# A hybrid decoder step on one core: projections summed over row quarters, h made by quarters, the last FFN round tile by tile

## The reference

```
mod = silu(c) @ w_ada + b_ada                      # c: 1 + 8 rows, w_ada 2048 x 12288
sh1, sc1, g1, sh2, sc2, g2 = split(mod, 6)
h = rmsnorm(x, g_pre_mix) * (1 + sc1) + sh1
z, xbc, dt, q, k, v = split(h @ w_in)              # 2048 x 5648
... conv and SSD mixer on z, xbc, dt; stick-breaking attention on q, k, v ...
m = concat(y, o) @ w_out                           # 2048 x 2048
x = x + g1 * rmsnorm(m, g_post_mix)
h = rmsnorm(x, g_pre_ffn) * (1 + sc2) + sh2
u = causal_conv(h @ w_ffn_in)                      # 2048 x 11264
f = (silu(gate(u)) * val(u)) @ w_ffn_out           # 5632 x 2048
x = x + g2 * rmsnorm(f, g_post_ffn)
```

## Time and profile before

| | us |
|---|---|
| median of three runs | 2014.4 (2013.41 to 2021.6) |
| profiled execution, time | 2012.36 |
| profiled execution, span from first to last instruction | 2010.4 |
| first projection product starts | 129.0 |
| output projection's last adaLN rows copied | 1077.4 |
| last product tile of the FFN added | 1975.0 |

### The profile page before, as it was taken

The page is one execution under the profiler, slowest core; times in us unless marked ns, Lnnn a source line. Parts: engine busy times, 40 slices in busy tenths (PEclk is TensorE's granted clock), DMA queues, the critical chain, the costliest instruction groups (busy, mean ns, idle before and its releaser), DMA issues.

```text
span 2010.4 us, 31591 instructions
## 1 busy us (share of the span) xinstructions
PE 1788.4 (89%) x13853; PEld 1584.5 (79%) x13853; DVE 942.2 (47%) x1212; ACT 653.1 (32%) x607; POOL 52.8 (3%) x146
## 2 busy tenths in 40 slices
PE   3869999997667887885997799999999999999986
PEld 2348998896545665453996799999999999999985
DVE  0052323323665332535234756566566566566554
ACT  1132222223633342113222543333333333333332
POOL 1000000000000000010000000000000000000001
PEclk9869999998678895587999899999999999999997
DMA  9966887884058993036674344444444454544431
GB/s 325 340 240 225 287 281 261 278 282 161 3 186 304 367 361 102 0 116 230 231 279 160 105 152 165 167 168 168 165 159 162 165 167 168 168 164 160 160 104 63
DMA packets 185180, 389.49 MB, mean 194 GB/s; under 512 B 9692, under 2 KB 18572, under 8 KB 184458
## 3 DMA queue, kind: packets, MB, share of 16 engines
q1 hardware_dynamic: 178816, 373.32, 53.8%
q0 software_dynamic: 2592, 10.42, 1.4%
q10 hardware_dynamic: 3634, 3.74, 0.6%
HBM read 377.03 MB, written 10.41 MB: 193 GB/s over the span
## 4 chain that ended last, share of the span: by engine, by line
PE 80%; DVE 9%; DMA 4%; ACT 4%; issue 2%; ACTq 1%; SPq 0%; POOL 0%; DVEq 0%; POOLq 0%
PE ps L667 20%; PE ps L668 20%; PE ps L669 20%; PE ps L623 4%; PE ps L642 4%; DMA araw<-in_w_ada_dram 2%; PE ps L864 2%; PE ps L735 1%; PE ps L1004 1%; ACTq L1163 1%; PE ps L897 1%; PE ps L631 1%; PE ps L995 1%; PE ps L1052 1%; DVE xraw L1676 1%
## 5 line engine op out<-in xcount | busy, mean ns | idle before, releaser
L1481 DVE TENSOR_TENSOR wlo<-raw,whi 128x2048 fp32r<-128x2048 f32 x192 | 438.2, 2289 | 441.3 <-ACT whi L1208 440.9
L1208 ACT ACTIVATE whi<-raw 128x2048 fp32r<-128x2048 f32 x192 | 367.0, 1915 | 665.1 <-PE ps L669 372.5
L667 PE MATMUL ps<-h2hi,whi 128*128 128x288 f32 x1408 | 416.7, 296 | 12.3 <-DVE wlo L1481 12.3
L668 PE MATMUL ps<-h2lo,whi 128*128 128x288 f32 x1408 | 417.4, 296 | 0.0
L669 PE MATMUL ps<-h2hi,wlo 128*128 128x288 f32 x1408 | 416.6, 296 | 0.0
L667 PEld LDWEIGHTS ps<-h2hi,whi 128*128 128x128 f32 x1408 | 268.2, 190 | 12.9 <-issue 11.9
L669 PEld LDWEIGHTS ps<-h2hi,wlo 128*128 128x128 f32 x1408 | 264.6, 188 | 0.0
L668 PEld LDWEIGHTS ps<-h2lo,whi 128*128 128x128 f32 x1408 | 264.5, 188 | 0.0
L667 PE MATMUL ps<-hhi,whi 128*128 128x288 f32 x704 | 211.5, 300 | 11.7 <-DVE wlo L1481 11.7
L667 PE MATMUL ps<-ghi,whi 128*128 128x288 f32 x704 | 209.0, 297 | 5.5 <-DVE wlo L1481 5.5
L668 PE MATMUL ps<-hlo,whi 128*128 128x288 f32 x704 | 210.5, 299 | 0.0
(11 more groups left out here) (373 smaller groups left out, 2122.1 us busy)
## 6 DMA issues: line engine op xcount, KB each, us to landing
raw<-in_w_ffn_in_dram SPq DMA_DIRECT2D x88, 1024.0 KB, 5.0
raw<-in_w_ada_dram SPq DMA_DIRECT2D x64, 1024.0 KB, 6.6
raw<-in_w_in_dram SPq DMA_DIRECT2D x44, 1024.0 KB, 8.5
raw<-in_w_ffn_out_dram SPq DMA_DIRECT2D x44, 1024.0 KB, 5.0
araw<-in_w_ada_dram SPq DMA_DIRECT2D x32, 1024.0 KB, 13.9
kring<-in_cache_k_dram SPq DMA_DIRECT2D x64, 512.0 KB, 5.8
vring<-in_cache_v_dram SPq DMA_DIRECT2D x64, 512.0 KB, 5.9
raw<-in_w_out_dram SPq DMA_DIRECT2D x16, 1024.0 KB, 5.8
```

What stands on the lines that cost most here:

```text
L667: mm(o, whi[:, high, q, cols], xh, start=(first and q == 0), stop=False)
L668: mm(o, whi[:, high, q, cols], xl, start=False, stop=False)
L1208: fn(whi[:, g % HIGH], raw[:, ring.slot[u]], ACT.Copy).then_inc(hi_ready, 1)
L1481: tt(wlo[:, slot], raw[:, slot], whi[:, g % HIGH].bitcast(F32), SUB).then_inc(lo_ready, 1)
```

## The change

- **Order of tiles.** 8 a, then four times (`ggaaa` five times and one g), 4 a, then `ggaaa` eight times, then g. The same 96 adaLN tiles and the same product tiles. `ADA_ORDER` sorts the first eight adaLN groups so that scale and shift of chunk quarter 0 come first, then those of quarter 1 and so on.
- **Products by row quarters.** The projection goes over all 11 groups with the rows of quarter 0, then of quarter 1, and so on (output projection: quarters 2, 3, 0, 1). Each product tile is complete in PSUM by itself. It uses two pairs of banks out of three (banks 0 to 5), p % 3; adaLN has bank 7 and the fold and the dt products bank 6. ACT copies the first quarter's pairs out, DVE adds the pairs of the three others into `proj` or `mT`.
- **h by quarters.** `hf` holds 4 chunks. Quarter 0 is made ahead of the first product, quarters 1 to 3 on DVE and ACT at adaLN tiles 16, 24 and 32; the dt products go along in four parts.
- **Start.** ACT issues c, x, then the vectors; POOL issues contexts, wdt and the rest. DVE's copies of the contexts come behind the norm.
- **Last round.** `ghi2`, `glo2` in buffers of their own; 16 tiles of one chunk each in banks 0 to 2; beside each the rows of x2 (x before the last sum, transposed), and gf = gain * f transposed; squares summed on DVE; then one multiply-add of rows with the norm's factor per token, and six stores on SP's queue.
- Some semaphores are merged; nothing else moves.

```diff
+    MIXER = ("ggaaa" * (PROJ_GROUPS // 2) + "g") * QUARTERS
+    OUTPUT = "ggaaa" * (QUARTERS * OUT_GROUPS // 2)
-    ring = Ring("a" * FIRST + "ggaa" * (PROJ // 4) + "a" * BETWEEN + "ggaa" * (RING * KC // MC // 2) + "g" * (3 * RING * FC // MC),
+    ring = Ring("a" * FIRST + MIXER + "a" * BETWEEN + OUTPUT + "g" * (3 * RING * FC // MC),
                 FIRST, WIDE, DEEP, (FIRST, BEFORE_OUT))
+    ADA_ORDER = [g for q in range(QUARTERS) for g in (QUARTERS + q, q)] + list(range(2 * QUARTERS, 6 * QUARTERS))
...
+            def product(x):
...
                 pe.wait_ge(lo_ready, g + 1)
                 for m in range(MC):
+                    p = 2 * g + m // 2
+                    if m % 2 == 0 and p >= 3:
+                        pe.wait_ge(*evacuated(p - 3))
+                    o = ps[:, 2 * (p % 3) + m % 2, 0:T]
+                    cols = slice(m * P, (m + 1) * P)
+                    for q in range(QC):
+                        xh, xl = x(product_of(g)[0] * QC + q)
+                        mm(o, whi[:, high, q, cols], xh, start=(q == 0), stop=False)
+                        mm(o, whi[:, high, q, cols], xl, start=False, stop=False)
+                        i = mm(o, wlo[:, slot, q, cols], xh, start=False, stop=(q == QC - 1))
...
+            def quarter(p):
+                dve.wait_ge(mod_ready, 2 * (p + 1))
+                c.link(stt(gainT[:, part], modT[:, SC1 + 4 * p:SC1 + 4 * p + 4, :], 1.0, vec, ADD, MUL))
+                if p:
+                    dve.wait_ge(dt_full, p)
+                    dve.wait_ge(h_hi, p)
+                    dve.wait_ge(h_lo, p)
+                tt(hf[:], xT[:, part], rT[:].unsqueeze(1).to_broadcast([P, QC, T]), MUL).then_inc(xr_ready, 1)
...
+                dve.wait_ge(h_hi, p + 1)
+                tt(hlo[:, part], hf[:], hhi[:, part].bitcast(F32), SUB).then_inc(h_lo, 1)
...
+            for kind in MIXER:
+                if kind == "a":
+                    ada(a)
+                    a += 1
+                else:
+                    q, g = product_of(n)
+                    if n + 1 < QUARTERS * PROJ_GROUPS:
+                        lo()
+                    if q:
+                        for i in range(2):
+                            from_psum(proj[:, MC * g + 2 * i:MC * g + 2 * i + 2, :], n, i)
+                    n += 1
...
+            for j in range(KC):
+                f_tile(j)
+                if j == 0:
+                    conv_rows()
+                if 1 <= j <= 12:
+                    if j == 1:
+                        pe.wait_ge(fc_o, 2)
+                    x2_rows(j - 1)
+                if j >= 3:
+                    gf_rows(j - 3)
+            for k in range(KC - 3, KC):
+                gf_rows(k)
...
+            for t in range(NT + 1):
+                w = P if t < NT else TS
+                r = rtok[0:w, t:t + 1]
+                early, late = x2tok[0:w, t, 0:DM - GC], x2tok[0:w, t, DM - GC:DM]
+                stt(early, gtok[0:w, t, :], r, early, MUL, ADD).then_inc(y_ready, 1)
+                stt(late, ps[0:w, 5 + t, :], r, late, MUL, ADD).then_inc(y_ready, 1)
```

More of the change, by code:

```diff
@@ L444, in _ @@
             sp.wait_ge(dtE_full, SC)
[L445 to L451, removed]
-            for i in range(KC // MC):
-                pair(w_out_v, i * GC, after_states if i == 0 else (lambda j: None))
+            for i in range(BETWEEN):
+                ada()
+            for half in range(2):
+                sp.wait_ge(hn_dma[half], 16 * (NB // 2))
+            for kind in OUTPUT:
+                if kind == "a":
+                    ada()
+                else:
+                    q, g = product_of(pos.g)
+                    load(rows(w_out_v, q, g * GC))
+                    pos.g += 1
             def fo(r):
@@ L645, in ada_unit @@
                 pos.u += 1
-            def adaq(bank, fold_last=True):
-                pe.wait_ge(group_free, pos.group + 1)
-                if fold_last:
-                    fold(bank)
-                for j in range(RING):
-                    ada_unit(bank, j)
                 pos.ada += 1
-            def unit3(bank0, xs, first, last, before=lambda m: None):
+            def product(x):
                 u, g = pos.u, pos.g
@@ L772, in _ @@
[L772 to L780 removed]
+            for i in range(RING):
+                ada()
+            pe.wait_ge(rows_out, 1)
+            pe.wait_ge(in_ctx, 32)
+            for n in range(11):
+                i = tr(ps[:, 1 + n // 4, (n % 4) * P:(n % 4 + 1) * P], frow[:, n, :], P)
@@ new lines, in _ @@
+            i.then_inc(rows_T, 1)
+            for n in range(3):
+                i = tr(ps[:, 4, n * 96:(n + 1) * 96], srow[0:96, n, :], 96)
+            i.then_inc(rows_T, 1)
+            fold()
+            pe.wait_ge(rows_out, 2)
+            pe.wait_ge(root_ready, 1)
+            for kind in MIXER:
+                if kind == "a":
+                    ada()
+                else:
+                    if pos.g % PROJ_GROUPS == 0:
+                        pe.wait_ge(h_lo, pos.g // PROJ_GROUPS + 1)
+                    product(lambda k: (hhi[:, k, :], hlo[:, k, :]))
@@ L1138, in _ @@
+            pe.wait_ge(tile_summed, KC)
+            for t in range(NT + 1):
+                w = P if t < NT else TS
+                i = mm(ps[0:w, 3, t:t + 1], fsum[:, t * P:t * P + w], ones[:, 0:1], start=True, stop=True)
+            i.then_inc(sum_ready, 1)
         @block.scalar
@@ new lines, in _, with ada @@
+            c.link(dve.reciprocal(rT[:], rT[:]))
+            rows_of()
+            mod_of()
+            rows_of()
+            contexts()
+            mod_of()
+            quarter(0)
+            lo()
+            def ada(a):
+                group, j = divmod(a, RING)
+                if j == 0 and group > pos.folded:
+                    mod_of()
+                if a in (16, 24, 32):
+                    quarter(a // 8 - 1)
+                if j == 3:
+                    if dts[0] < QUARTERS and group == 2 * (dts[0] + 1):
+                        dt_part()
+                    rows_of()
@@ new lines, in _ @@
+            for j in range(KC):
+                if j in (1, 3, 5):
+                    lo()
+                if j in (7, 11, 15):
+                    rows_of_gf((j - 7) // 4)
+                tile(j)
+                if j:
+                    total(j - 1)
+            total(KC - 1)
+            norms[0] += 1
+            dve.wait_ge(root_ready, norms[0])
+            dve.reciprocal(rtok[:, 0:NT], rtok[:, 0:NT])
+            c.link(dve.reciprocal(rtok[0:TS, NT:NT + 1], rtok[0:TS, NT:NT + 1]))
```

675 lines of the change are left out of this document (391 added, 284 removed).

## The result

The changed kernel takes **2077.1 us** (median of 4 runs, 2071.0 to 2079.0), the kernel before 2015.0 beside it: a ratio of 1.030, 95% interval 1.027 to 1.033. The prediction was 1990, with a range of 1972 to 2012. The change is slower by 62 us where 24 less were forecast.

A forecast was written before the change was run, and what follows sets the result against it. PE was taken to wait for loads at the start and to be the bound itself from the first projection product. Projection -23, output projection +14 and last round -15.6 give -24: 2014.4 to 1990 us, range 1972 to 2012.

The forecast's parts named there:

- Folds: Projection stage: half of the folds stand right behind their group's last tile, PE waits 0.86 us for row copies, 7 us.
- the item on the sums: Projection stage: DVE adds 66 pairs of banks, 50 us, beside PE, at no cost unless DVE stands at a split.
- Start: Before the first projection product: small loads leave ACT's queue, 8 adaLN tiles stand ahead; product at 66 us, 63 earlier.
- Projection stage: First projection product to last fold: 366 us of work plus waits, 389 in all, ending at 455 instead of 477.5.
- late tiles: Projection stage: a pair's first product tile, queued behind four loads, lands late, 0.3 us per cycle, 5 us over 16 cycles.
- it just fits: Projection stage: a product tile landing in 5.0 us is loaded and split in 9.4, within a cover of 9.9 to 10.3.
- The quarters: Projection stage: making a quarter of h between DVE's splits delays the next split, three times 3.5 us, 10.5 in all.
- Output stage: Output projection: eight more adaLN tiles, two more folds, waits at folds and late tiles, together 14 us longer.
- Tail: Last FFN round and end: no idle PE at 1940, last tile at 1979.5, end at 1994.8, 15.6 us less.
- Rival 3: Projection stage: product tiles land later than 7.2 us, so cycles lengthen and the kernel is slower, above 2014; chance 0.09.
- Rival 2: Start bound by another thing, first product at 76, and quarters cost 18 us: 17 more, 2007; chance 0.19.
- Rivals 1 and 4: 1: loads keep up, start 6 us earlier, 1972, chance 0.20; 4: DVE's order holds PE until 129, 2053, chance 0.02.

The follow-up runs named there:

- Run 1: Changed kernel with the copy of finished adaLN rows made by ACT ahead of its next split, no longer by DVE, in both projections: 2028.0 us, ratio 1.005.
- run 8: Changed kernel with DVE's row copy ahead of the next product's split where a group ends inside a run, projection stage only: 2035.9 us, ratio 1.010.
- Run 6: Changed kernel with useless matmuls ahead of seven projection-stage folds, so PE is not idle while the row copy is awaited: 2057.4 us, ratio 1.021.
- run 9: Changed kernel with DVE's row copies ahead of the split in both stages and dt products one adaLN group later: 2013.9 us, ratio 1.000.
- run 5: Kernel before with only the changed last FFN round and tail, and the merged semaphores of the middle: 1998.3 us, ratio 0.992.
- run 2: Changed kernel with adaLN tiles behind the first two groups loading half their rows, used twice: 2069.5 us, ratio 1.025.

## Why the prediction was wrong

**The step that failed is "Folds"**: "PE then waits for the row copy, 0.86 before such folds of the start. 8 x 0.86 = 7." Measured in the projection stage of the changed kernel: 33.9 us at ten folds. The 0.86 was read at a place where DVE had nothing else to do. In the stage the copy is third in a queue that begins with a split, and the order in the code said so. The same slip is in the item on the sums: they "cost nothing, unless DVE stands at a split that waits for its tile; that wait is the one already counted". It was counted for the product that needs the tile; nobody asked who else was queued behind the waiting split. The forecast's own numbers would have given it: 5.0 + 1.9 + 2.3 for the split, 1.4 for two sums and 0.7 for the copy are 11.3, against 6.5 + 0.95 at which a group that ends with a run's first tile wants its fold: 3.9 us, and 2.9 where it ends with the second. Measured 3.6 to 4.9 and 1.5 to 3.0. And it is two folds in three, not half; five of each kind make 34 us by these numbers. Run 1 moved the copy to another engine (-49) and run 8 moved it within its own (-41): both ways show this cause.

**The clock** behind such waits was no term at all. PE's waits in the stage come to some 49 us (33.9 at folds, 9.2 at dt products, the rest at splits) where 22.5 were forecast. Without them it still takes 395 us where the prediction had 366 of work: some 29 us more, most of it slower matmuls. Run 6 shows the clock as a price of its own, some 2.8 us per wait. The Trainium skill, TensorE: Matmul & The Clock Gate, section "What's actually happening", states that the gate passes either half or all of the pulses, by how busy PE has been; the windows of 0.50 and 1.00 and run 6 agree.

**What was right, or off in size**, from run 9, where the failed step is mended:
- Start: predicted 66, measured 73.5. The order of steps was right. In the changed kernel the first four adaLN tiles were through at 29.8, not at 24 to 26 (its eight first loads landed after 18.5 us, median), and sums, four tiles and fold ran in part at the lower clock, 9.69 + 6.25 + 1.76 for 8.0 + 3.7 + 1.0. The prediction had 74 as its bound, for another reason.
- Projection stage: predicted 389, 402.1 in run 9. Its ten copies wait 0.81 each, 8 us for the 7 forecast. The first products of pairs wait 4.0 us in all for late tiles, 5 forecast: "it just fits" held. The quarters cost 1.97 + 3.35 + 3.94 at the split behind them, 9.3 for 10.5. What was left out is 3.05 for the dt products behind a fold, and slower products (8.18, 9.34 and 8.91 for 6.67 us behind waits, and one of 8.21 behind a wait of only 0.14), 8 us together. Some 3 us of the stage stay unaccounted for.
- Output stage: +14 predicted, +33.9 in the changed kernel, +16.8 in run 9.
- Tail: predicted -15.6; -17.3 in the traces and -16.0 in run 5's median. Right, by its mechanism: no idle PE at the last round, its last tile added 39.5 us after its first product (39.4 forecast), the end 13 after (15 forecast).

The misses of run 9 are 7.5 + 13.1 - 0.2 + 2.8 - 1.6 = 21.6; its span is 2007.9, and 2010.4 - 24 is 1986.4, 21.5 less. So with the folds mended the prediction would still have been too fast, and 2013.9 lies just outside its range: the start gains 55 us, the projection stage gives back 54 and the output stage 17, a loss of some 15 that the tail's 17 little more than make good. Run 5, the tail without all this, is 15.6 us faster than run 9.

**The rivals.** None named this mechanism. Rival 3, the slower one with the most weight (0.09), expected landings above 7.2; they were 5.2, and halving the adaLN loads (run 2) changed little. The Trainium skill, DMA: Bandwidth & Descriptors, section "Anatomy of one DMA — SWDGE (gpsimd) path", gives for POOL's path an estimate of 4.4; these loads are issued by SP, and their trace has 5.2. Rival 2 was near on the start (76), but its 18 for the quarters did not come: 9.3 in run 9. Rivals 1 and 4 did not happen.

**What stays open**: the best place of the dt products, since the same edit gained on run 1 and cost on run 8; whether the start could be 66 with a full clock, which was not tried; and why the attention's pages, at a lower clock, and the FFN take 7 to 8 us longer in some profiles. The runs of one kernel spread as widely, run 9's from 2001.8 to 2025.1 (10 runs); what makes them differ is not known.

## What to carry to other kernels

When a step is said to wait "for a copy of 0.7 us", write down what stands ahead of that copy on its engine, and when each of those is ready; an instruction that waits for a load is a wait for everybody behind it in the queue, not for its own consumer alone. Put short instructions that release the bound engine ahead of long ones that wait for loads, and price a gap of PE with the slower matmuls behind it. Make separable parts of a change one by one: here the tail was a gain (-16), the issue of small loads too (4.5 us at the first product), and the large part, with its queue orders mended, still cost some 16 us (run 9 against run 5).

## What the runs showed of the hardware

- The granted TensorE clock fell to its lower level behind waits of 3 to 5 us inside a stage that is else full: fold 1.88 for 0.95 us, 16 adaLN matmuls 3.64 for 1.92, the next 96 product matmuls up to 14.9 for 13.1. Behind waits of 0.81 the fold took 1.06 and the tiles 1.92. Useless matmuls in the gap kept it up and made the kernel 19.7 us faster.
- Between these the same wait can go either way. In the changed kernel the clock fell behind a wait of 1.75 us (fold 1.60, granted clock 0.50 at 136 to 140 us), not behind one of 1.50. Ahead of the same product it fell in run 9 behind 1.97 us (0.50 at 140.7 to 142.7, product 8.18) and stayed at 1.00 in run 8 behind 2.26 (product 6.69). The fall can come some 2 us after PE has gone on: behind the wait of 2.87 us at 1060.75 in the changed kernel's output stage it was still 1.00 up to 1062.7, and 0.61 from there to 1065.
- ACT stood 19.39 us at the issue of a small load before. With the same loads issued by POOL, ACT was through at 7.8 us and POOL needed 0.5 to 1.2 us for each.
- Stages of the same instructions took two lengths in different profiled executions: the FFN up to its last `up` 838 to 839 or 844 to 845 us.
